# Attention layers' weights split ahead of time, kept in DRAM and loaded back as finished tiles by GpSimd's queue

## The reference

```
for l in range(2):
    h = rmsnorm(x, attn_norm[l])
    proj = einsum('bsd,de->bse', h, w_in[l])            # 1024 -> 3*512 + 3*512
    sb_q, sb_k, sb_v, df_q, df_k, df_v = split(proj)
    sb_out = stick_breaking_attention(sb_q, sb_k, sb_v)  # 8 heads of 64
    dq, dk = rope(df_q), rope(df_k)
    df_out = rmsnorm(differential_attention(dq, dk, df_v, lam), subln[l]) * (1 - lambda_init)
    x = x + einsum('bse,ed->bsd', concat(sb_out, df_out), w_o[l])
    h = rmsnorm(x, mlp_norm[l])
    u = square(relu(einsum('bsd,df->bsf', h, w_ff1[l])))  # 1024 -> 4096
    x = x + einsum('bsf,fd->bsd', u, w_ff2[l])
```

## Time and profile before

| what | value |
|---|---|
| runs shown | 2709.89, 2710.25, 2710.47 us |
| span of the profiled execution | 2708.0 us |
| PE busy | 2687.0 us, 99% of the span |
| DVE, ACT, POOL busy | 57%, 43%, 25% |
| moved by DMA | 236.73 MB through SP's queue, 28.1% of 16 engines' span |
| attention 0, 1462 to 1744 us | PE busy 278.61 of 282.00 us |
| attention 1, 2081 to 2361 us | PE busy 276.89 of 280.00 us |

### The profile page before, as it was taken

The page is one execution under the profiler, slowest core; times in us unless marked ns, Lnnn a source line. Parts: engine busy times, 40 slices in busy tenths (PEclk is TensorE's granted clock), DMA queues, the critical chain, the costliest instruction groups (busy, mean ns, idle before and its releaser), DMA issues.

```text
span 2708.0 us, 32235 instructions
## 1 busy us (share of the span) xinstructions
PE 2687.0 (99%) x12902; PEld 2250.4 (83%) x12902; DVE 1551.6 (57%) x2312; ACT 1154.0 (43%) x1836; POOL 681.2 (25%) x695
## 2 busy tenths in 40 slices
PE   8999999999999999999999999999999999999999
PEld 7888888888888888888888888788888888788887
DVE  6656554344466646665575668644445558655444
ACT  4323423222347636532235767522224667522223
POOL 1000111011136626400004753411103553511100
PEclk9999999999999999999999999999999999999999
DMA  4332232323222222223322221233333211233332
GB/s 160 97 101 93 91 108 93 101 95 100 90 75 61 67 75 67 86 95 101 100 94 88 82 67 40 79 101 97 98 94 103 78 57 54 71 101 94 97 98 78
DMA packets 69414, 238.80 MB, mean 88 GB/s; under 512 B 7696, under 2 KB 10256, under 8 KB 69264
## 3 DMA queue, kind: packets, MB, share of 16 engines
q1 hardware_dynamic: 69264, 236.73, 28.1%
HBM read 234.60 MB, written 2.10 MB: 87 GB/s over the span
## 4 chain that ended last, share of the span: by engine, by line
PE 91%; DVE 4%; POOL 2%; ACT 2%; issue 0%; DMA 0%; SPq 0%; ACTq 0%; DVEq 0%
PE ps L416 29%; PE ps L418 29%; PE ps L417 29%; POOL wl L2419 2%; PE ps L552 1%; PE ps L777 1%; PE ps L776 1%; PE ps L485 0%; DVE wl L1636 0%; ACT wh L1018 0%; PE ps L613 0%; PE ps L612 0%; DVE xl L1648 0%; PE ps L470 0%; PE ps L452 0%
## 5 line engine op out<-in xcount | busy, mean ns | idle before, releaser
L1018 ACT ACTIVATE wh<-raw 128x1024 fp32r<-128x1024 f32 (+2 forms) x453 | 465.2, 1028 | 730.7 <-PE ps L418 723.7
L416 PE MATMUL ps<-xh,wh 128*128 128x512 f32 x1920 | 751.7, 391 | 0.2 <-POOL wl L2419 0.2
L418 PE MATMUL ps<-xh,wl 128*128 128x512 f32 x1920 | 747.4, 389 | 0.0
L417 PE MATMUL ps<-xl,wh 128*128 128x512 f32 x1920 | 747.2, 389 | 0.0
L1636 DVE TENSOR_TENSOR wl<-raw,wh 128x1024 fp32r<-128x1024 f32 (+1 forms) x339 | 447.7, 1321 | 156.9 <-ACT wh L1018 156.5
L416 PE MATMUL ps<-yh,wh 128*128 128x512 f32 x1088 | 425.3, 391 | 1.9 <-POOL wl L2419 1.9
L416 PEld LDWEIGHTS ps<-xh,wh 128*128 128x128 f32 x1920 | 360.5, 188 | 76.2 <-issue 1.0
L417 PE MATMUL ps<-yl,wh 128*128 128x512 f32 x1088 | 423.5, 389 | 0.0
L418 PE MATMUL ps<-yh,wl 128*128 128x512 f32 x1088 | 423.4, 389 | 0.0
L418 PEld LDWEIGHTS ps<-xh,wl 128*128 128x128 f32 x1920 | 360.4, 188 | 75.1
L417 PEld LDWEIGHTS ps<-xl,wh 128*128 128x128 f32 x1920 | 360.6, 188 | 74.8 <-issue 1.0
(11 more groups left out here) (267 smaller groups left out, 3628.6 us busy)
## 6 DMA issues: line engine op xcount, KB each, us to landing
raw<-in_ff SPq DMA_DIRECT2D x120, 512.0 KB, 3.6
raw<-in_pool_in SPq DMA_DIRECT2D x64, 512.0 KB, 3.3
raw<-in_conv_in SPq DMA_DIRECT2D x64, 512.0 KB, 3.3
raw<-in_pool_out SPq DMA_DIRECT2D x32, 512.0 KB, 3.3
raw<-in_qk SPq DMA_DIRECT2D x32, 512.0 KB, 3.7
raw<-in_pool_grp SPq DMA_DIRECT2D x16, 512.0 KB, 3.3
raw<-in_conv_out SPq DMA_DIRECT2D x16, 512.0 KB, 3.3
raw<-in_mla_z SPq DMA_DIRECT2D x16, 512.0 KB, 3.6
```

Source lines behind the costliest of these rows:

```text
L416: pe.do.matmul(o, lh, rh_, start=start, stop=False)
L417: pe.do.matmul(o, lh, rl_, start=False, stop=False)
L418: return pe.do.matmul(o, ll, rh_, start=False, stop=stop)
L1018: act.do.activation(h[:, 0:ncol], r[:, 0:ncol], ACT.Copy).then_inc(*mark("whi", ("whi", k)))
```

## The change

The 64 attention units of the last two layers are split in earlier stages: those of layer 0 in the convolution (one after every two of its units), those of layer 1 in feed-forward 0 (four after every seven). For each, SP loads the raw unit into the raw ring, ACT rounds it into a staging tile (PTH or DFH in turn), DVE makes the low half in PTL or DFL, and SP stores both to a DRAM tensor `split`, float32, 512 KB each. In the attention layers SP, ACT and DVE (or POOL) do nothing for these units; POOL issues two DMAs per unit, from `split` to WH and WL, as soon as the WH/WL pair is free. These DMAs convert float32 to float32r. `low(True)` and `low(False)` around the attention units are gone, so no unit of them and none of f1 is flagged for POOL.

Beside this, the identity and the ones come with `strict` into OB, and `const` shrinks from 579 to 323 columns; the sums of uses 1 and 5 are split in G[0] and G[1]; four readers of the staging tiles wait for the last stores; and the ring for DMA descriptors is larger.

```
@@ unit_table
-        low(True)
-        for kind, *key in LAYER_UNITS:
+        start, every = (("cc", 0), (1, 8)) if l == 0 else (("f1", 0, 0, 0), (8, 7))
+        for j, (kind, *key) in enumerate(LAYER_UNITS):
+            early[len(units)] = (l, j)
+            steps[index[start] + every[0] + every[1] * j // 4] = (l, j, len(units))
...
-                if qd == 0 and i == 0:
-                    low(False)
...
+    loads = []
+    for n in range(len(units)):
+        if n not in early:
+            loads.append(n)
+        if n in steps:
+            loads.append(steps[n])
@@ program
+        def stage(j):
+            hi, lo = (DFH, DFL) if j % 2 else (PTH, PTL)
+            return hi[:, 0:WN], lo[:, 0:WN]
@@ ACT
+                    if k in steps:
+                        split(*steps[k])
+            def split(l, j, n):
+                act.wait_ge(*at("raw", n))
+                if j > 1:
+                    act.wait_ge(*at("kept", l, j - 2))
+                elif l:
+                    act.wait_ge(*at("mm", "pv", 0, "d" if j else "s", 3 if j else 7))
+                act.do.activation(stage(j)[0], raw[loads[l, j, n][0]][:, :], ACT.Copy).then_inc(
+                    *mark("act", ("parth", l, j)))
@@ DVE
+            def split(l, j, n):
+                hi, lo = stage(j)
+                dve.wait_ge(*at("parth", l, j))
+                dve.do.tensor_tensor(lo, raw[loads[l, j, n][0]][:, :], f(hi), ALU.subtract).then_inc(
+                    *mark("dve", ("partl", l, j)))
@@ POOL, weights
+                    if k in early:
+                        pool.wait_ge(*at("kept", *early[k]))
+                        pool.wait_ge(*at("wfree", k - NSPLIT))
+                        src, slot = D["split"][early[k]], f"split{k % NSPLIT}"
+                        pool.do.dma_start(WH[k % NSPLIT][:, :], src[0]).then_inc(*mark(slot, by=16))
+                        pool.do.dma_start(WL[k % NSPLIT][:, :], src[1]).then_inc(*mark(slot, ("wlo", k), by=16))
+                        continue
@@ SP
+            def load(key, n):
+                slot, before = loads[key]
+                src, ncol, _, _ = units[n]
+                if isinstance(before, tuple):
+                    l, j, _ = before
+                    hi, lo = stage(j)
+                    sp.wait_ge(*at("partl", l, j))
+                    sp.do.dma_start(D["split"][l, j, 0], f(hi)).then_inc(*mark(f"kept{j % 2}", by=16))
+                    sp.do.dma_start(D["split"][l, j, 1], f(lo)).then_inc(*mark(f"kept{j % 2}", ("kept", l, j), by=16))
+                elif before is not None:
+                    sp.wait_ge(*at("wlo", before))
+                sp.do.dma_start(raw[slot][:, 0:ncol], src).then_inc(*mark(f"raw{slot}", ("raw", n), by=16))
@@ host
+    D["split"] = nc.dram_tensor("split", (2, 32, 2, 128, WN), F32, kind="Internal").ap()
```

More of the change, by code:

```diff
@@ L118, in unit_table @@
 def unit_table(D):
-    units, index, lows = [], {}, False
+    units, index, early, steps = [], {}, {}, {}
     def add(key, src, ncol, dup=False):
@@ L208, in unit_table @@
         u.append(on)
-    return units, index
+    loads = []
[4 more added lines that the diff above has]
+            loads.append(steps[n])
+    return units, index, early, steps, {key: (i % NRAW, loads[i - NRAW] if i >= NRAW else None)
+                                        for i, key in enumerate(loads)}
 def temp_table():
@@ L319, in program @@
         sems = {n: ctx.enter_context(nc.semaphore(f"s_{n}")) for n in SEMS}
-        units, unit = unit_table(D)
+        units, unit, early, steps, loads = unit_table(D)
         temps = temp_table()
@@ L325, in f @@
             return ap.bitcast(F32)
-        ident = const[:, C_ID:C_ID + 128]
-        ones = const[:, C_ONE:C_ONE + 128]
+        ident, ones = f(identr[:, :]), f(onesr[:, :])
         m_caus = const[:, C_CAUS:C_CAUS + 128]
         m_chunk = const[:, C_CHUNK:C_CHUNK + 128]
-        m_before, m_after = OB[:, 0:128], OB[:, 128:256]
+        m_before, m_after, ident_in, ones_in = (OB[:, k * 128:k * 128 + 128] for k in range(4))
         eps = const[:, C_EPS:C_EPS + 1]
@@ L450, in sum_squares @@
                 pe.wait_ge(*at(*last_square(use)))
-                pe.wait_ge(*at("const"))
+                pe.wait_ge(*at("ones"))
                 pe.do.matmul(b[:, :], ones, ACC[:, :], start=True, stop=True).then_inc(
@@ L1010, in weights @@
                         act.wait_ge(*at("wfree", k - NSPLIT))
-                    r, h = raw[k % NRAW], WH[k % NSPLIT]
+                    r, h = raw[loads[k][0]], WH[k % NSPLIT]
                     if dup:
@@ L1622, in weights, with low_weights @@
                     made[0] += 1
+                    if k not in early:
+                        low_weights(k)
+                    if k in steps:
+                        split(*steps[k])
+            def split(l, j, n):
[3 more added lines that the diff above has]
+                    *mark("dve", ("partl", l, j)))
+            def low_weights(k):
                     _, ncol, dup, on_pool = units[k]
                     if on_pool:
-                        continue
+                        return
                     dve.wait_ge(*at("whi", k))
-                    r, h, lo = raw[k % NRAW], WH[k % NSPLIT], WL[k % NSPLIT]
+                    r, h, lo = raw[loads[k][0]], WH[k % NSPLIT], WL[k % NSPLIT]
                     if dup:
@@ L2637, in weights @@
                     made[0] += 1
[L2638 to L2642, removed]
+                    if k not in early:
+                        load(k, k)
+                    if k in steps:
+                        load(steps[k], steps[k][2])
+            def load(key, n):
[10 more added lines that the diff above has]
+                sp.do.dma_start(raw[slot][:, 0:ncol], src).then_inc(*mark(f"raw{slot}", ("raw", n), by=16))
             sp.do.dma_start(vec[:, :], D["vec"]).then_inc(*mark("vec", ("vec",), by=16))
```

33 lines of the change are left out of this document (19 added, 14 removed).

## The result

The changed kernel takes 2747.71 us, median of four runs (2745.95 to 2748.25), against 2710.24 before: a ratio of 1.0138, 95% interval 1.0124 to 1.0152, so 37.5 us slower. The prediction was 2730.2 with a range of 2718 to 2746, so the time lies 1.7 us above the range. The direction was right and the place of the largest loss was right; the size forecast, 20.0 us, is about half of what came.

A forecast was written before the change was run, and what follows sets the result against it. The prediction took PE, busy for 2687.0 of 2708.0 us, to bound the kernel. Its terms, −2.3 + 14.1 + 4.1 + 4 = +19.9, gave a span of 2727.9 and a time of 2730.2 us, range 2718 to 2746.

The forecast's parts named there:

- The loads: Attention layers: GpSimd's loads of finished halves come late at four places, +4.1 us; line 416's waits for POOL go, −2.3.
- L: Time from a free buffer to both of GpSimd's loads landed, taken as 5.4 us, between 4.2 and 7.4.
- The last output units: Last two output units of both layers: buffers free 5.0 and 4.8 us before need, loads 5.4, +1.0 a layer.
- The fifth unit of attention 0: Its load, issued after the first scaling of x, lands at 1489.9 and is late: +1.9 us.
- The clock: After PE's long idle at each attention layer's end, matmuls run at 1.2 GHz: 2 us a layer, +4 (0 to 6.6).
- The rival of no clock drop: The same forecast without the +4 for slower matmuls: 2726.2 us, chance 0.15.
- The end of each attention layer: DVE makes f1(0) and f1(1)'s low halves after the last xl, so `first_pair` starts 7.0 and 7.1 us later: +14.1.
- Splitting early: Convolution and feed-forward 0: extra splits raise DVE to some 71% and traffic to some 255 GB/s, at cost 0.
- the rival of crowded stages: Split work or stores hold up the convolution or feed-forward 0: +19 on top, 2749 us, chance 0.06.
- Slow loads: Rival: GpSimd's loads in the attention layers take 7.4 us or more, +12: 2742.2 us, chance 0.13.
- No gain: Rival of a gain: f1's two low halves don't hold PE and attention waits go, at most 6.5 us: 2703.8, chance 0.04.
- The 0.24% bound on any gain: PE idles only 6.5 us in the two attention layers, so the change cannot win more there.

The follow-up runs named there:

- e3: The changed kernel with the ring for GpSimd's DMA descriptors doubled from 512 to 1024 bytes, nothing else: 2740.78 us.
- e7: e6 with POOL issuing the loads of two more units before its part of turning dk(3), in each attention layer: 2711.48 us.
- e6: e5 with the splits for layer 1 starting three units earlier in feed-forward 0: 2713.01 us.
- e4: The kernel before with one part of the change alone, f1(0) to f1(2) of both layers lowered by DVE instead of POOL: 2733.97 us.
- e11: The changed kernel with POOL adding the squares at each attention layer's end only after DVE made f1(1)'s low half: 2739.34 us.
- e8: Built like e5, but no attention unit split ahead or stored; POOL loads each unit's raw weights into both tiles: 2711.30 us.
- e9: e7 with the splits for layer 1 starting at the twelfth unit of feed-forward 0, in denser steps: 2707.80 us.
- e1: The changed kernel with f1(0) to f1(2) of both layers again given to POOL for their low halves: 2722.38 us.
- e2: The changed kernel with DVE making the low halves of f1(0) and f1(1) before the xl of blocks 2 and 4: 2723.72 us.
- e5: The changed kernel with the edits of e1 and e3 together: 2714.84 us.

## Why the prediction was wrong, and where it was right

The forecast was 17.7 us short of the span, and its terms were, in us:

| term | forecast | measured |
|---|---|---|
| PE's waits before the pairs, less the 2.6 of before | +14.1 | +17.1 |
| PE's waits for loads, less the 2.3 of before | +1.8 | +9.0 |
| slower matmuls | +4 | +10.9 |
| splitting early: the wait for yl | 0 | +1.5 |
| opening and small waits | 0 | −0.9 |
| sum | +19.9 | +37.6 |

Two terms were about 7 us too small each, the loads and the clock; the waits before the pairs, where the mechanism was right, were 3.0 us too small.

**The loads** (+4.1 with L = 5.4, against 2.3 that went). L was a little high: 4.9. PE's waits were 11.3 us. The step "Most units have 10 us between the release of their buffer and PE's need. Four places have not" failed: it took the other units as safe by the slack of their buffers, and did not ask what POOL and SP do when these come free. Two things had no term in the sum. One is the ring, which the diff told by the number 512 and no row could price: POOL stood up to 5.7 us before an issue, and it cost 6.9 us with the clock behind it (e3). The other is where POOL comes late to a load because of its own work (e7), or where SP's loads and stores are under way beside POOL's (10.7 us to landing in the changed kernel, 8.0 in e6). The last output units, forecast at 1.0 a layer, were 0.9 and 1.0 late. The fifth unit of attention 0, forecast at +1.9, was 0.4 us earlier than before: the scaling of x in front of its load ended at 1483.30 in place of 1484.5, and the load took less than 5 us.

**The clock** (+4, 0 to 6.6). Right for the pairs, 3.9 us together; wrong in seeing only them. 68 matmuls lost 11.5 us, 7.4 of it inside the attention layers, behind waits of 1.8 to 3.2 us and in one place behind none over 0.3. The step "the longest idle time later in the trace is 1.28 us, with no slow matmul behind it" says nothing of waits between 1.28 us and the opening's 6.46, and the changed kernel has four of those at its loads and at yl; three of them have slow matmuls behind them. The rival of no clock drop fell: the granted clock behind the pair's wait is 0.50. What it leaned on, a granted clock of 1.00 at the opening beside matmuls 0.43 us apart, is explained by no run. The 7.4 us are also those of one execution: where a stretch of the clock falls varies, as the last point of this document shows.

**The end of each attention layer** (+14.1 forecast, bounds 5.7 to 8.9 a layer). Mechanism right, size too small: the pairs start 8.6 and 8.5 us later in the changed kernel, near the upper bound, and 9.5 each when it is done alone in e4, above it. The step that was off is "Two low halves at 1.23 us": that duration is from feed-forward 0, where POOL hardly works, and the step then took 0.4 off because POOL's pieces would be gone. They took 4.4 us and not 2.1. The last xl came 0.9 us earlier than the sum had it, measured from the last matmul of the output product, and hid a part of that. The cause is POOL's adding of squares, which goes on beside DVE there (e11). Its cost to DVE could have been read: the xl beside it took 1.35 us each and 0.75 at the shortest, and the pair of low halves 1.97. The chosen value should have been that last one, since it was the row of the same place; it gives 8.9 a layer.

**Splitting early** (0 forecast). Close: 3.5 us by e8, 1.5 of it one wait for yl behind a split on DVE, the rest mostly the late load at attention 1's start. The traffic came as forecast, 250 and 253 GB/s for 255. PE stayed at 50.00 of 50.00 us in the two windows shown, so the rival of crowded stages fell.

**The rivals.** Slow loads did not come as a rule: the median landing is 4.3 us with DVE busy for 190 of 282 us, and the landings over 7 us stand at the starts of the two layers, beside SP's loads. The Trainium skill, "SBUF — State Buffer" (the "DVE blocks DMA" trap), was named for this rival; it speaks of DVE operations in a two-port mode, with a float32 copy from SBUF to SBUF as its example, and no run here sets such a copy beside a load. The estimate of near 8 us for L that was worked out from its figure stands against a median of 4.9. No gain came, since PE waited for DVE, POOL's ring and the loads instead. The 0.24% bound on any gain held: e9, with 3.2 us of waits for loads left, is 0.1% under the kernel before. One event was in neither the forecast nor its rivals: a queue that stands although its buffers are free.

## What to carry to other kernels

When an edit drops a flag or moves work to another engine, read the order of that engine at the stage's end and ask what stands in front: here three units a layer, a side effect beside the 32 that the change is about, made two thirds of the loss, and either of two other places would have left no wait. Take a duration from the row of the same place with the same neighbour, not from the group's mean. And when loads move to a queue with a ring of descriptors, count how many are in flight when several buffers come free at once, and what else the engines of the DMA carry then.

## What the runs showed of the hardware

- POOL's 128 x 512 additions slow DVE's operations with two inputs from SBUF by nearly a factor of two: wl 2.23 us beside them and 1.16 without, xl 1.36 and 0.70 (e11 against the changed kernel). POOL's additions take 9.60 / 5 = 1.92 us there and 1.29 at 2094.54.
- With a ring of 512 bytes at most three loads of 512 KB that GpSimd issued were under way at once, and the second load of a unit was never issued before both loads of the unit before had landed; with 1024 bytes up to six were under way, and the idle time before the issues fell from 39.1 to 9.2 us (e3). By what rule the ring comes free is not shown.
- A load of 512 KB by GpSimd's queue, with conversion from float32 to float32r, took 3.6 us (first) and 4.3 us (second of a pair) to landing, median, against 3.7 by SP in the kernel before, and 0.53 us of POOL to issue. Beside four raw loads and two stores of SP it took up to 10.7.
- The granted clock also fell where PE had hardly been idle. The same window of the changed kernel, and then of the kernel before:

```profile
1625.00:1630.00 5.00, 5.00 (x28) 4.00 (x28) 3.92 (x12) 4.90 (x12) 0.00 (x0) 0.73 0.00 0
```

```profile
1625.00:1630.00 5.00, 4.95 (x33) 4.09 (x34) 3.59 (x8) 4.91 (x11) 0.00 (x0) 1.00 0.00 0
```

PE is busy for nearly all of both, among matmuls of small tiles, and at 0.73 in one and 1.00 in the other. e11 and e1 issue the same matmuls as the changed kernel up to there; the same window of e11, and then of e1:

```profile
1625.00:1630.00 5.00, 5.00 (x30) 3.97 (x29) 3.92 (x11) 4.91 (x11) 0.00 (x0) 0.77 0.00 0
```

```profile
1625.00:1630.00 5.00, 5.00 (x32) 3.88 (x31) 4.34 (x15) 4.94 (x12) 0.00 (x0) 1.00 0.00 0
```

It is 1.00 in e2 to e5 as well. So the drop there, 10 matmuls and 1.8 us, does not hang on the change alone and comes in some executions and not in others; what decides stays open, and no run was made for it.
